# The forget heads of a mixer: probabilities normalised before their turn, values as the stationary operand

## The chip, the cores and the metric

The kernel runs on one core of a Trainium2 chip. The metric is device time in microseconds (us) of one execution. TensorE (PE in the rows) multiplies, VectorE (DVE) and ScalarE (ACT) do elementwise work and move results out of PSUM, GpSimd (POOL) and SyncE (SP) have small parts here; SP issues nearly all weight loads.

## What is computed

Two blocks, one behind the other, on 256 tokens of width 1024. The first block has two layers. Each layer has a mixer with three groups of heads: four differential heads ("diff", eight softmax units of 128 values), four forget heads ("fox", 64 values each) and four retention heads. Then comes a feed-forward part, dense in layer 0 and a mixture of eight experts in layer 1. Only the forget heads change:

```python
def causal_block_attention(q, k, v, scale, cum_logf=None):
    ...
        s = jnp.einsum('bhqd,bhkd->bhqk', q_i, k).astype(jnp.float32) * scale
        if cum_logf is not None:
            s = s + blk[2][..., :, None] - cum_logf[:, :, None, :]
        s = jnp.where(k_pos[None, :] <= q_pos[:, None], s, NEG_INF)
        w = jax.nn.softmax(s, axis=-1).astype(v.dtype)
        return jnp.einsum('bhqk,bhkv->bhqv', w, v)
...
    o_b = merge_heads(causal_block_attention(qb, kb, vb, FOX_DIM ** -0.5, cum))
    return jnp.concatenate([o_a, o_b, o_c], axis=-1) @ w_out
```

## The kernel before, in words

Weights arrive as pieces of 1 MB. ScalarE rounds each piece to a high part (`split`, L1479), VectorE subtracts to get a low part (L2040), and every wide product is three matmuls, high by high, low by high, high by low (`exact`, L758 to L760). Three pieces are held in parts at once; an engine asks for the next piece in program order (`splits`). Each engine runs its own program strictly in its written order and waits on semaphores.

The mixer of a layer is in `attention1`, once per engine, and runs the twelve units of `RUN1` (eight diff units, then fox 0 to 3) as a software pipeline with the step number `i`. On TensorE, step `i` issues the scores of units `i` and `i+1` (at even `i`), turns the probabilities of unit `i-1` (`turn`, L873, three transposes), multiplies unit `i-2` with its values (`values`, L882), and then, up to step 9, a part of a projection (`rows_half` or `feature`, L758 to L760). On VectorE, step `i` takes the row maxima of unit `i` (L2222), at steps 3, 5, 7, 9 finishes a diff head (`diff_out`, L2241 to L2246), at step 9 rotates the retention heads' queries and keys (L2395 to L2400), at step 10 scales the diff rows (L2269), and up to step 8 ends with the low part of a piece (L2040). On ScalarE, step `i` makes the exponentials and row sums of unit `i` (`exps`, L1587), copies the turned probabilities of unit `i-1` out of PSUM (`copy_turned`, L1597), and up to step 10 ends with the high part of a piece (L1479).

Behind the pipeline come the retention heads: scores (`ret_score`, L994, L995), weights made on VectorE (`weigh`, L2299) behind one more low part, and `ret_values` (L1002 to L1005), which wait for `weigh`. The rows of the mixer's result, `y1`, are turned in four blocks of 256 features (`turn_y`, L729; blocks 0 and 1 diff, 2 fox, 3 retention), taken as high and low parts (`turned_y`), and multiplied with the output weights (`output(l, c, j)`, twelve matmuls of L758 to L760 each, for block `c` and column half `j`). Behind step 13, `mixed` issues what is left of them.

For a fox unit, before the change: the exponentials stay unnormalised, are turned, and are then the stationary operand of three products per unit with 64 columns of values moving. The result has tokens on the partitions; when all four units are done, VectorE takes the reciprocals (L2311), scales the whole bank into `y1` (L2312), and TensorE turns these rows with `turn_y(l, 2)`.

## Time and profile before

| | us |
|---|---|
| median of 3 runs | 1936.92 |
| lowest, highest | 1936.78, 1942.82 |
| profiled execution, its own time | 1937.35 |
| its span | 1935.6 |
| PE busy | 1901.9 (98%) |
| VectorE busy, ScalarE busy | 1517.2 (78%), 1261.2 (65%) |
| mean granted TensorE clock | 0.997 |

The mixers' last parts lie at 96 to 140 us (layer 0) and 448 to 493 us (layer 1) of the span. In a timeline row the start says when the first instruction of the row began; matmuls are pipelined, so the step from one row's start to the next one's is what a row takes of TensorE's time, and the length printed is longer than that. The clock column is the granted clock as a share of full speed, 1.00 for 2.4 GHz and 0.50 for 1.2 GHz.

### The profile page before, as it was taken

How to read it: one execution, taken by the hardware profiler on the slowest of the kernel's cores; microseconds unless marked ns; L12 is line 12 of the kernel's file. 1: busy time of each engine (PE TensorE's matmuls, PEld its weight loads, DVE VectorE, ACT ScalarE, POOL GpSimd, SP SyncE). 2: the span in 40 equal slices, each digit the busy share in tenths (PEclk: the TensorE clock that was granted, in tenths of full speed). 3: DMA queues.
4: the chain of work that ended last, by engine and by line, in shares of the span. 5: the costliest groups of instructions: out<-in, count | busy, mean ns of one | idle time of the engine just before them, and what ended most of it. 6: DMA issues, size and time to landing. Idle time of an engine off the chain costs nothing.

```text
span 1935.6 us, 28198 instructions
## 1 busy us (share of the span) xinstructions
PE 1901.9 (98%) x10499; PEld 1614.6 (83%) x10499; DVE 1517.2 (78%) x1792; ACT 1261.2 (65%) x1678; POOL 40.4 (2%) x30
## 2 busy tenths in 40 slices
PE   8999999999899999999999999999999999999999
PEld 7879998888688888888888888888877788788977
DVE  5575555657789989899898989989898875878575
ACT  5654544555777878787787778878777556454553
POOL 0000000000000000000000000000120000000000
PEclk9999999999999999999999999999999999999999
DMA  7717555430899999999999999999996553355421
GB/s 249 250 49 263 180 190 175 153 131 15 315 366 383 365 389 364 391 386 366 393 360 391 366 390 387 364 392 363 390 398 231 172 175 109 131 174 178 149 88 45
DMA packets 246215, 514.38 MB, mean 266 GB/s; under 512 B 12516, under 2 KB 59368, under 8 KB 246120
## 3 DMA queue, kind: packets, MB, share of 16 engines
q1 hardware_dynamic: 242936, 502.48, 72.1%
q0 software_dynamic: 2896, 10.49, 1.4%
q8 instruction: 64, 1.05, 0.2%
q14 instruction: 31, 0.25, 0.0%
q10 hardware_dynamic: 288, 0.11, 0.0%
HBM read 507.27 MB, written 5.77 MB: 265 GB/s over the span
## 4 chain that ended last, share of the span: by engine, by line
PE 85%; DVE 9%; ACT 3%; DMA 1%; issue 1%; ACTq 0%; DVEq 0%
PE bank L758 26%; PE bank L760 26%; PE bank L759 26%; DVE low L2040 2%; DVE low L2640 2%; PE bank L729 1%; PE bank L1180 1%; PE bank L882 1%; DMA scr<-expert_rows,kept_row 1%; ACT high L1479 1%; PE bank L873 1%; PE bank L851 1%; DVE atD L2851 1%; DVE kT L2875 0%; DVE qT L2874 0%
## 5 line engine op out<-in xcount | busy, mean ns | idle before, releaser
L2640 DVE TENSOR_TENSOR low<-raw,high 128x1024 fp32r<-128x1024 f32 x672 | 783.8, 1220 | 72.9 <-ACT high L1683 71.3
L1683 ACT ACTIVATE high<-raw 128x1024 fp32r<-128x1024 f32 x336 | 357.3, 1063 | 206.7 <-PE bank L760 202.2
L2040 DVE TENSOR_TENSOR low<-raw,high 128x2048 fp32r<-128x2048 f32 (+1 forms) x138 | 310.4, 2259 | 164.5 <-ACT high L1479 164.1
L1479 ACT ACTIVATE high<-raw 128x2048 fp32r<-128x2048 f32 (+1 forms) x138 | 260.6, 1894 | 158.6 <-PE bank L760 147.3
L758 PE MATMUL bank<-high,xg_hi 128*128 128x512 f32 x896 | 353.6, 395 | 1.3 <-DVE xg_lo L2620 1.3
L1684 ACT ACTIVATE high<-raw 128x1024 fp32r<-128x1024 f32 x336 | 351.7, 1047 | 0.0
L760 PE MATMUL bank<-high,xg_lo 128*128 128x512 f32 x896 | 349.5, 390 | 0.0
L759 PE MATMUL bank<-low,xg_hi 128*128 128x512 f32 x896 | 348.8, 389 | 0.0
L758 PE MATMUL bank<-high,xT_hi 128*128 128x512 f32 (+1 forms) x576 | 227.4, 395 | 2.5 <-DVE xT_lo L2062 1.3
L760 PE MATMUL bank<-high,xT_lo 128*128 128x512 f32 (+1 forms) x576 | 221.5, 385 | 0.0
L759 PE MATMUL bank<-low,xT_hi 128*128 128x512 f32 (+1 forms) x576 | 221.1, 384 | 0.0
L758 PE MATMUL bank<-high,hT_hi 128*128 128x512 f32 x536 | 209.7, 391 | 1.7 <-DVE hT_lo L2652 1.7
L759 PE MATMUL bank<-low,hT_hi 128*128 128x512 f32 x536 | 208.7, 389 | 0.0
L760 PE MATMUL bank<-high,hT_lo 128*128 128x512 f32 x536 | 208.7, 389 | 0.0
L760 PEld LDWEIGHTS bank<-high,xg_lo 128*128 128x128 f32 x896 | 168.2, 188 | 35.8
L758 PEld LDWEIGHTS bank<-high,xg_hi 128*128 128x128 f32 x896 | 168.2, 188 | 35.1 <-issue 1.6
L759 PEld LDWEIGHTS bank<-low,xg_hi 128*128 128x128 f32 x896 | 168.4, 188 | 33.8
L758 PE MATMUL bank<-xT_hi,high 128*128 128x256 f32 x672 | 192.4, 286 | 3.5 <-issue 1.9
L759 PE MATMUL bank<-xT_lo,high 128*128 128x256 f32 x672 | 190.8, 284 | 0.0
L760 PE MATMUL bank<-xT_hi,low 128*128 128x256 f32 x672 | 190.8, 284 | 0.0
L758 PEld LDWEIGHTS bank<-xT_hi,high 128*128 128x128 f32 x672 | 129.6, 193 | 5.0 <-issue 2.2
L759 PEld LDWEIGHTS bank<-xT_lo,high 128*128 128x128 f32 x672 | 129.6, 193 | 0.4
(357 smaller groups left out, 2309.9 us busy)
## 6 DMA issues: line engine op xcount, KB each, us to landing
raw<-in_moe_w_gate SPq DMA_DIRECT2D x112, 1024.0 KB, 8.9
raw<-in_moe_w_up SPq DMA_DIRECT2D x112, 1024.0 KB, 8.6
raw<-in_moe_w_down SPq DMA_DIRECT2D x112, 1024.0 KB, 8.2
raw<-in_w_in SPq DMA_DIRECT2D x63, 1024.0 KB, 5.3
raw<-in_w_out SPq DMA_DIRECT2D x20, 1024.0 KB, 5.0
raw<-in_dense_w_gate SPq DMA_DIRECT2D x11, 1024.0 KB, 5.4
raw<-in_dense_w_up SPq DMA_DIRECT2D x11, 1024.0 KB, 5.3
raw<-in_dense_w_down SPq DMA_DIRECT2D x11, 1024.0 KB, 5.1
```

The costliest lines, as they stand in the source:

```text
L729: last = pe.transpose(bank_of(key)[:, (k * NT + t) * P:(k * NT + t + 1) * P], rows[:, t, (2 * j + k) * P:(2 * j + k + 1) * P], ident[:, :])
L758: pe.matmul(dst, stationary[0], moving[0], start=start, stop=False)
L759: pe.matmul(dst, stationary[0], moving[1], start=False, stop=False)
L760: return pe.matmul(dst, stationary[1], moving[0], start=False, stop=stop)
L851: pe.matmul(bank[(g + i) % 2][:, c0:c0 + n], q[:, tok(t)], k[:, 0:n], start=(t == 0), stop=False)
L873: last = pe.transpose(bank[2 + g % 2][:, b * P:(b + 1) * P], probs[:, g % 2, b * P:(b + 1) * P], ident[:, :])
L882: last = pe.matmul(att_out(name, u, t), probsT[:, g % 2, c0 + s * P:c0 + (s + 1) * P], val[:, s, :], start=(s == 0), stop=(s == n // P - 1))
L1479: act.activation(high[:, slot, 0:k * n], raw[:, raw_slot[piece], 0:k * n], ACT.Copy).then_inc(high_done, 1)
L1683: act.activation(part[:, 0:HALF // 2], raw[:, slot, 0:HALF // 2], ACT.Copy).then_inc(s["high_half"], 1)
L1684: act.activation(part[:, HALF // 2:HALF], raw[:, slot, HALF // 2:HALF], ACT.Copy).then_inc(s["high"], 1)
L2040: dve.tensor_tensor(low[:, slot, 0:k * n], src, high[:, slot, 0:k * n].bitcast(F32), ALU.subtract).then_inc(low_done, 1)
L2640: last = dve.tensor_tensor(low_part[:, cols], raw[:, at0 + k % slots, cols], high_part[:, cols].bitcast(F32), ALU.subtract)
```

## The change

The four fox units are handled in another way. VectorE normalises each unit's probabilities in place (`fox_rows`: a reciprocal of two row sums, and two in-place scalings of 128x128 and 128x256), and `turn` of a fox unit now waits for that (`fox_scaled`) instead of for the exponentials. The values of two units are multiplied together (`fox_values`): a unit's values are the stationary operand, 64 columns wide, and its turned probabilities move, 256 and 128 columns; one unit writes partitions 0 to 63 of bank 4 and the other 64 to 127. The result already has features on the partitions, so the scaling into `y1` (L2311, L2312), the mark behind it and `turn_y(l, 2)` go, and the block is read from bank 4. On ScalarE, the high part of that block is moved ahead of the gate's Silu. The numbers of two semaphores are counted anew.

```diff
--- before.py
+++ after.py
@@ -418,7 +419,7 @@
             unit(("qcT", l), "act", on=6)
             unit(("kcT", l), "act", on=7)
             for j in range(4):
-                unit(("yT", l, j), "dve", on=(0, 0, 6, 7)[j])
+                unit(("yT", l, j), "dve", on=(0, 0, 4, 7)[j])
             chunk(("wo", l), rows_of(io["w_out"][l], 0, KB))
             if l == 0:
                 places = plan_front(("ffn", l), [("dg", 0), ("du", 0)], True, 4)
@@ -510,7 +511,6 @@
                 att_first[name, l], att_n = att_n, att_n + n
             for k in range(4):
                 out_use["diff", l, k] = len(out_use)
-            out_use["fox", l] = len(out_use)
             out_use["ret", l] = len(out_use)
             out_use["wo", l] = len(out_use)
             if l == 0:
@@ -866,7 +866,11 @@
 
             def turn(name, g):
                 spans = att_shape(name)[2]
-                pe.wait_ge(att_exp, g + 1)
+                if name == "fox":
+                    fox_no = g - att_first["fox", 0]
+                    pe.wait_ge(fox_scaled, fox_no + 1 if fox_no < 4 else g - att_first["fox", 1] + 5)
+                else:
+                    pe.wait_ge(att_exp, g + 1)
                 if g >= 2:
                     pe.wait_ge(att_copied, g - 1)
                 for b in range((spans[1][0] + spans[1][1]) // P):
@@ -882,6 +886,19 @@
                         last = pe.matmul(att_out(name, u, t), probsT[:, g % 2, c0 + s * P:c0 + (s + 1) * P],
                                          val[:, s, :], start=(s == 0), stop=(s == n // P - 1))
                 last.then_inc(att_pv, 1)
+
+            def fox_values(l, p):
+
+
+                turned = att_first["fox", l] + 2 * p
+                pe.wait_ge(att_copied, turned + 2)
+                for s in range(NT):
+                    for i in range(2):
+                        cols = slice(0, SEQ) if s == 0 else slice(SEQ, 3 * P)
+                        last = pe.matmul(bank[4][64 * i:64 * i + 64, p * SEQ + s * P:(p + 1) * SEQ],
+                                         v[:, s, 512 + 64 * (2 * p + i):576 + 64 * (2 * p + i)],
+                                         probsT[:, (turned + i) % 2, cols], start=(s == 0), stop=(s == NT - 1))
+                last.then_inc(*((att_pv, 2) if p == 0 else (unit_full, 1)))
 
             def attention1(l):
 
@@ -915,9 +932,13 @@
                             pe.wait_ge(out_taken, out_use["diff", l, max(0, u // 2 - 1)])
                             if u == 4:
                                 emptied(pe, ("forgetT", l))
-                        if (name, u) == ("fox", 0):
-                            pe.wait_ge(out_taken, out_use["diff", l, 3])
-                        values(name, u, first + i - 2)
+                        if name == "diff":
+                            values(name, u, first + i - 2)
+                        elif u % 2 == 1:
+                            if u == 1:
+                                pe.wait_ge(out_taken, out_use["diff", l, 3])
+                                free_bank(pe, ("yT", l, 2))
+                            fox_values(l, u // 2)
                     if i < 10:
                         name = ("va", "vfb", "qkb", "qkc", "vgc")[i // 2]
                         if name == "qkb":
@@ -941,7 +962,7 @@
                         pe.wait_ge(att_exp, first + 11)
                         turn_y(l, 0)
                     if i == 12:
-                        pe.wait_ge(out_taken, out_use["fox", l])
+                        pe.wait_ge(out_taken, out_use["ret", l])
                         ret_values(l, 0)
                         ret_values(l, 1)
                         ret_score(l, 2)
@@ -953,6 +974,8 @@
                         output(l, 0, 0)
                 ret_values(l, 2)
                 ret_values(l, 3)
+                filled(pe, ("yT", l, 2))
+                pe.nop().then_inc(att_pv, 2)
 
             def attention2(l):
 
@@ -1006,7 +1029,7 @@
                           start=False, stop=True).then_inc(ret_pv, 1)
 
             def turn_y(l, j):
-                pe.wait_ge(y_ready, 3 * l + max(1, j))
+                pe.wait_ge(y_ready, 2 * l + (2 if j == 3 else 1))
                 turn_rows(("yT", l), y1, [j])
 
             def output(l, c, j):
@@ -1032,7 +1055,6 @@
                 output(l, 1, 0)
                 pe.wait_ge(att_copied, att_first["fox", l] + 4)
                 output(l, 0, 1)
-                turn_y(l, 2)
                 output(l, 1, 1)
                 emptied(pe, ("yT", l, 2))
                 output(l, 2, 0)
...
@@ -1916,11 +1938,11 @@
                 attention1(l)
 
                 turned_y(l, 1)
+                turned_y(l, 2)
                 emptied(act, ("vgc", l, 1))
                 act.activation(sg[:, :, :], sg[:, :, :], ACT.Silu).then_inc(gates_in, 1)
                 sqrt_ahead()
                 serve_sqrt(8)
-                turned_y(l, 2)
                 splits(pieces_of["wo", l][0])
                 turned_y(l, 3)
                 splits(last_piece["wo", l] - 1)
@@ -2247,12 +2269,25 @@
                                                         in1=ya[:, t, hd, :], op0=ALU.mult, op1=ALU.add)
                     last.then_inc(out_taken, 1)
 
+                def fox_rows(u):
+
+
+                    dve.wait_ge(att_exp, att_first["fox", l] + u + 1)
+                    r = rinv[:, 2 * u:2 * u + 2]
+                    link(dve.reciprocal(r, rowsum[:, 2 * u:2 * u + 2]))
+                    for t, (c0, n) in enumerate(att_shape("fox")[2]):
+                        rows = probs[:, (att_first["fox", l] + u) % 2, c0:c0 + n]
+                        last = dve.tensor_scalar(rows, rows, r[:, t:t + 1], None, ALU.mult)
+                    last.then_inc(fox_scaled, 1)
+
                 for i in range(len(RUN1)):
                     if i == 5:
                         take_scaled(("qkb", l, 0), qT[:, 4:6, :], 0.125)
                     if i == 6:
                         take_scaled(("qkb", l, 1), kT[:, 4:6, :])
                     maxima(*RUN1[i], first + i)
+                    if i >= 9:
+                        fox_rows(i - 9)
                     if i in (3, 5, 7, 9):
                         diff_out((i - 3) // 2)
                     if i == 5:
@@ -2299,6 +2334,7 @@
                     dve.tensor_tensor(ret_w[:, u, :], bank[6 + u % 2][:, 0:3 * P], decay[:, u, :],
                                       ALU.mult).then_inc(ret_weights, 1)
 
+                fox_rows(3)
                 splits(pieces_of["vgc", l][0])
                 weigh(0)
                 weigh(1)
@@ -2307,14 +2343,7 @@
                 weigh(2)
                 weigh(3)
                 turned_y(l, 1)
-                dve.wait_ge(att_pv, first + len(RUN1))
-                link(dve.reciprocal(rinv[:, 0:8], rowsum[:, 0:8]))
-                dve.tensor_tensor(y1[:, :, 512:768].rearrange("p t (h n) -> p h t n", h=4),
-                                  bank[4][:, :].rearrange("p (h t n) -> p h t n", h=4, t=NT),
-                                  per(rinv[:, 0:8].rearrange("p (h t) -> p h t", h=4), 64),
-                                  ALU.mult).then_inc(out_taken, 1)
-                dve.wait_ge(out_taken, out_use["fox", l] + 1)
-                mark().then_inc(y_ready, 1)
+                turned_y(l, 2)
 
             def attention2(l):
 
@@ -2476,7 +2505,6 @@
                 ycf = y1[:, :, 768:1024]
                 dve.wait_ge(gates_in, l + 1)
                 dve.tensor_tensor(ycf, ycf, sg[:, :, :], ALU.mult).then_inc(y_ready, 1)
-                turned_y(l, 2)
                 splits(pieces_of["wo", l][0])
                 turned_y(l, 3)
                 splits(last_piece["wo", l] - 2)
```

VectorE, steps 9 and 10 of layer 0, from the maxima of fox 1 on. Before:

```order
L2222 TENSOR_REDUCE negmax<-bank 128x1
L2241 RECIPROCAL rinv<-rowsum 128x4 [waits att_pv]
L2242 TENSOR_SCALAR rinv<-rinv,lam 128x2 [waits dve_step]
L2244 TENSOR_TENSOR yf<-bank,rinv 128x2x128 [waits dve_step]
L2246 SCALAR_TENSOR_TENSOR yf<-bank,rinv,yf 128x128 [waits dve_step]
L2246 SCALAR_TENSOR_TENSOR yf<-bank,rinv,yf 128x128
L2105 TENSOR_SCALAR stat<-ysum 128x8 [waits diff_squares_summed]
```

The same place in the change:

```order
L2244 TENSOR_REDUCE negmax<-bank 128x1
L2277 RECIPROCAL rinv<-rowsum 128x2 [waits att_exp]
L2280 TENSOR_SCALAR probs<-probs,rinv 128x128 [waits dve_step]
L2280 TENSOR_SCALAR probs<-probs,rinv 128x256
L2263 RECIPROCAL rinv<-rowsum 128x4 [waits att_pv]
L2264 TENSOR_SCALAR rinv<-rinv,lam 128x2 [waits dve_step]
L2266 TENSOR_TENSOR yf<-bank,rinv 128x2x128 [waits dve_step]
L2268 SCALAR_TENSOR_TENSOR yf<-bank,rinv,yf 128x128 [waits dve_step]
```

The normalisation of fox 0 stands behind the maxima of fox 1 and ahead of the last diff head.

VectorE, from the maxima of fox 3 on, before (`low` is the low part of a piece, `ret_w` the retention weights):

```order
L2222 TENSOR_REDUCE negmax<-bank 128x1 [waits att_scores]
L2222 TENSOR_REDUCE negmax<-bank 128x1
L2040 TENSOR_TENSOR low<-raw,high 128x2048 [waits high_parts_done]
L2299 TENSOR_TENSOR ret_w<-bank,at 128x384 [waits ret_scores] x2
L2062 SCALAR_TENSOR_TENSOR xT_lo<-bank,y_gain,xT_hi 128x256 [waits high_rows_taken]
```

In the change:

```order
L2244 TENSOR_REDUCE negmax<-bank 128x1 [waits att_scores]
L2244 TENSOR_REDUCE negmax<-bank 128x1
L2277 RECIPROCAL rinv<-rowsum 128x2 [waits att_exp]
L2280 TENSOR_SCALAR probs<-probs,rinv 128x128 [waits dve_step]
L2280 TENSOR_SCALAR probs<-probs,rinv 128x256
L2277 RECIPROCAL rinv<-rowsum 128x2 [waits att_exp]
L2280 TENSOR_SCALAR probs<-probs,rinv 128x128 [waits dve_step]
L2280 TENSOR_SCALAR probs<-probs,rinv 128x256
L2062 TENSOR_TENSOR low<-raw,high 128x2048 [waits high_parts_done]
L2334 TENSOR_TENSOR ret_w<-bank,at 128x384 [waits ret_scores] x2
L2084 SCALAR_TENSOR_TENSOR xT_lo<-bank,y_gain,xT_hi 128x256 [waits high_rows_taken]
```

The low part and the retention weights now stand behind the normalisation of fox 3, which waits for its exponentials.

TensorE, the turn of fox 3 and what follows, before:

```order
L873 MATMUL bank<-ident,probs 128x128 [waits att_copied,att_exp]
L873 MATMUL bank<-ident,probs 128x128 x2
L882 MATMUL bank<-v,probsT 128x64 [waits att_copied]
L882 MATMUL bank<-v,probsT 128x64 x2
L1002 MATMUL bank<-v,ret_w 128x64 [waits ret_weights,out_banks_taken]
```

In the change:

```order
L877 MATMUL bank<-ident,probs 128x128 [waits att_copied,fox_rows_scaled]
L877 MATMUL bank<-ident,probs 128x128 x2
L1025 MATMUL bank<-v,ret_w 128x64 [waits ret_weights,out_banks_taken]
```

The values of fox 2 are gone from here; the first retention product, with its wait for the weights, follows the turn at once.

## Rows read from the trace of the kernel before

**Rows 1.** The page, busy time of each engine.
```profile
PE 1901.9 (98%) x10499; PEld 1614.6 (83%) x10499; DVE 1517.2 (78%) x1792; ACT 1261.2 (65%) x1678; POOL 40.4 (2%) x30
```

**Rows 2.** Timeline of TensorE, layer 0; columns: start us, us, instruction, idle before.
```profile
96.10 0.49 PE L873 MATMUL bank<-ident,probs 128*128 128x128 f32 x3
...
102.66 0.93 PE L851 MATMUL bank<-kT,qT 64*128 64x128 f32 x8
103.51 1.58 PE L858 MATMUL bank<-yf,ident 128*128 128x128 f32 x8
104.92 0.39 PE L863 MATMUL bank<-causal,ident_one 128*128 128x128 bf16 x4
...
111.64 0.55 PE L873 MATMUL bank<-ident,probs 128*128 128x128 f32 x3 [1.09 <-ACT probs L1587]
...
112.74 0.39 PE L1002 MATMUL bank<-v,ret_w 128*128 128x64 f32 x2
...
115.45 0.47 PE L758 MATMUL bank<-high,xT_hi 128*128 128x512 f32 x1
...
118.30 0.78 PE L882 MATMUL bank<-v,probsT 128*128 128x64 f32 x6
118.91 0.39 PE L1002 MATMUL bank<-v,ret_w 128*128 128x64 f32 x2
...
125.80 0.60 PE L729 MATMUL bank<-ident,yf 128*128 128x128 f32 x4
126.16 0.48 PE L758 MATMUL bank<-high,xT_hi 128*128 128x512 f32 x1
```

**Rows 3.** Timeline of VectorE, layer 0.
```profile
96.03 2.29 DVE L2040 TENSOR_TENSOR low<-raw,high 128x2048 fp32r<-128x2048 f32 x1 [3.17 <-ACT high L1479]
...
98.78 0.17 DVE L2241 RECIPROCAL rinv<-rowsum 128x4 f32<-128x4 f32 x1
...
105.24 0.62 DVE L2222 TENSOR_REDUCE negmax<-bank 128x1 f32<-128x128 f32 x2
105.78 1.22 DVE L2269 TENSOR_TENSOR yf<-yf,stat 128x1024 f32<-128x1024 f32 x1
...
107.44 2.28 DVE L2040 TENSOR_TENSOR low<-raw,high 128x2048 fp32r<-128x2048 f32 x1
109.99 1.02 DVE L2299 TENSOR_TENSOR ret_w<-bank,at 128x384 f32<-128x384 f32 x2 [0.27 <-PE bank L995]
```

**Rows 4.** Timeline of ScalarE, layer 0.
```profile
108.34 0.65 ACT L1576 ACTIVATE kT<-bank 128x512 f32<-128x512 f32 x1
108.82 1.97 ACT L1479 ACTIVATE high<-raw 128x2048 fp32r<-128x2048 f32 x1
110.62 0.42 ACT L1587 ACTIVATE probs<-bank,negmax 128x128 f32<-128x128 f32 x1
```

**Rows 5.** Groups of VectorE by line and form: busy us, mean ns.
```profile
L2841 DVE TENSOR_SCALAR kT<-kT,lbs 128x256 f32<-128x256 f32 x8 | 2.7, 340 | 0.0
```

**Rows 6.** Timeline of layer 1, TensorE and VectorE.
```profile
448.05 0.49 PE L873 MATMUL bank<-ident,probs 128*128 128x128 f32 x3
...
450.75 0.17 DVE L2241 RECIPROCAL rinv<-rowsum 128x4 f32<-128x4 f32 x1
```

**Rows 7.** Timeline of TensorE, second block, products 64 columns wide side by side.
```profile
1644.85 1.15 PE L1358 MATMUL bank<-qT,kT 128*64 128x64 f32 x32
1645.93 0.50 PE L758 MATMUL bank<-high,xT_hi 128*128 128x512 f32 x1
```

**Rows 8.** Stretches: busy us of PE, PEld, DVE, ACT, POOL; clock; DMA share; GB/s.
```profile
11.80:15.20 3.40, 3.40 (x19) 3.40 (x18) 2.33 (x6) 2.90 (x5) 0.00 (x0) 0.51 1.10 348
...
466.40:468.70 2.30, 2.30 (x13) 1.92 (x13) 2.02 (x3) 0.00 (x0) 0.00 (x0) 0.50 0.00 0
```

**Rows 9.** Timeline of TensorE, the idle time ahead of the two low stretches.
```profile
10.55 0.35 PE L758 MATMUL bank<-xT_hi,high 128*128 128x256 f32 x1 [1.90 <-issue]
...
463.62 0.55 PE L873 MATMUL bank<-ident,probs 128*128 128x128 f32 x3 [1.08 <-ACT probs L1587]
```

More of the change, by code:

```diff
@@ L311, in program @@
         gates_in = sem("hgrn_gates_in")
+        fox_scaled = sem("fox_rows_scaled")
         hid_high, hid_ready = sem("hidden_high_ready"), sem("hidden_ready")
@@ L1387, in hgrn @@
                 heads(bank[4 + 2 * ((LEVELS + 1) % 2)], 0, 1).then_inc(hg_scores, 1)
-                pe.wait_ge(y_ready, 3 * LAYERS + 2 * l + 1)
+                pe.wait_ge(y_ready, 2 * LAYERS + 2 * l + 1)
                 turn_rows(("yT2", l), y2, (0, 1))
@@ L1437, in after_experts @@
                         if c == 3:
-                            pe.wait_ge(y_ready, 3 * LAYERS + 2 * l + 2)
+                            pe.wait_ge(y_ready, 2 * LAYERS + 2 * l + 2)
                             turn_rows(("yT2", l), y2, (2, 3))
```

## The prediction

> **What bounds the kernel now.** I read the page first: TensorE is busy 98% of the span [rows 1]. It is so by its own matmuls nearly everywhere, so whatever makes TensorE wait, or work longer, is paid in full. Then I went to the timeline of the one place that the change touches, the last steps of the mixer's pipeline, in layer 0 and in layer 1. Three things are to be seen there. TensorE turns fox 0 at 96.10 without idle time ahead of it, and waits only once in the tail, 1.09 us for the exponentials of fox 3 [rows 2]. VectorE is late against it: the low part of a piece starts at 96.03 because VectorE stood 3.17 us waiting for the high part, and only at 98.78 is VectorE through with the maxima of fox 1 [rows 3]. Layer 1 is the same picture, turn at 448.05, VectorE free at 450.75 [rows 6]. So TensorE is ahead of VectorE by 2.7 us at this point, and that costs nothing now because the turn of fox 0 needs only ScalarE.
>
> **The change, part by part**, in the times of layer 0.
>
> *Work taken off TensorE.* The four transposes of block 2 go: 125.80 to 126.16, 0.36 us, and with the shorter first matmul behind them some 0.44 [rows 2]. The values of a fox unit took 0.61 (118.30 to 118.91) [rows 2], 1.2 for two. Two units in the new form stream 768 columns. Full width, as many columns took 1.41 us (L858, 103.51 to 104.92); in two row halves of the array at once 0.85 (L851, 102.66 to 103.51) [rows 2]. Column halves are used elsewhere: 32 records of 64 columns in 1.08 us, 34 ns each [rows 7], against 0.10 us for a record of `values` (six in 0.61) [rows 2], so halves do overlap. I take 0.85, with 0.6 and 1.41 as ends: 0.35 less for each pair. The first pair stands where TensorE will wait anyway, so it is worth nothing. The second takes the place of one unit's 0.61 behind `output(l, 0, 0)`: 0.24 more there (0 to 0.8). On the path: 0.24 - 0.44 = -0.2 a layer.
>
> The Trainium skill, "TensorEngine Tiling (Array Packing)", section "Theoretical Speedup", states up to 2x for a small dimension of 64. By it and the new column count the pair would take half of 1.41, and the text's sum would be lower by 0.15 us a layer; rows 7 agree with an overlap.
>
> *Work taken off VectorE.* The reciprocals, the scaling of the bank and the mark go, about 1 us behind the last piece of the pipeline. VectorE's chain for the retention rows then starts when the last retention product is done, and the turn of block 3 comes four `output` blocks later; cover enough, I cost it at nothing.
>
> *Work put on VectorE.* A normalisation is a reciprocal of 0.17 [rows 3] and two scalings in SBUF, at most 0.34 each [rows 5]; pipelined I take 0.75. There are four a layer, and what counts is where they stand.
>
> *First wait.* The turn of fox 0 now needs the normalisation that follows the maxima of fox 1: 98.78 + 0.75 = 99.5, against 96.10. TensorE stops for 3.4 to 3.5 us with the values of diff 7, half of the last projection piece and the next scores queued behind it. In layer 1 it is 450.75 + 0.75 against 448.05, again 3.5. The diff head behind it on VectorE shifts by 1.6, its rotation ends at about 107.3 instead of 105.2, which the later scores hide.
>
> *What follows.* The scores of fox 2 came 2.58 us after 102.66 (maxima at 105.24) [rows 2, 3]; now 106.16 + 2.58 = 108.7. Maxima 0.54, normalisation of fox 1 0.75: the turn of fox 1 at 110.0, a second wait of about 1.2. Then L2269 (1.13 to the next), maxima of fox 3, normalisation of fox 2: 112.4, a third wait, about 1. ScalarE cannot make the exponentials of fox 3 before two moves of turned retention rows and a high part. TensorE's eight transposes (0.11 each by rows 2) end at 111.4, the second move (0.5) at 111.9, the high part (108.82 to 110.62, 1.8 us) at 113.7, the exponentials 1.02 later (110.62 to 111.64) at 114.8 [rows 2, 4]. Normalisation of fox 3: 115.5, where the turn was at 111.64.
>
> *The one that ends last.* VectorE's next instruction is the low part of a piece, and only then come the retention weights. Before, the low part ran at 107.44, under everything else, and the weights at 109.99 [rows 3]. Now it is behind fox 3: 115.5 + 2.2 = 117.7, first weights 118.25, first retention product at 118.3 against 112.74 [rows 2]. From there to `output(l, 0, 0)` it was 2.71 us (112.74 to 115.45) [rows 2], and nothing in it waits for more. So TensorE is 5.56 us late there, and dense behind it. With the -0.2 of above: **5.4 us a layer, 10.7 for both**.
>
> *The clock.* The granted clock stood at 1.2 GHz (0.51, 0.50) in two stretches shown, 11.8 to 15.2 and 466.4 to 468.7 [rows 8]; before the first TensorE had been idle 1.90 us, before the second 1.08 us in a stretch of short matmuls [rows 9]. In layer 0 the same 1.09 us brought no fall. A stop of 3.5 us is longer than any of these, and the second group of waits adds about 5 us of idle in 10. A stretch like 11.8 to 15.2 costs dense matmuls half of 3.4, so up to 1.7 us. I take 1.2 for the first stop of each layer (part of the slow time may fall on waits) and 1.2 for the second group; layer 1 has its slow stretch already, 1.2 to 1.7 us of loss, so there the second is no addition: 1.2 + 1.2 + 1.2 = 3.6, less 0.5 for the chance that one stays away, **3.1**. The ends are -1.7 (none anywhere, the present one gone as well) and +8 (two or three in each layer, fully paid).
>
> The Trainium skill, "TensorE: Matmul & The Clock Gate", section "What's actually happening", calls the throttled clock the default state that activity releases; the 0.51 behind 1.90 us of idle time agrees. By this rule the sum keeps the clock's part; without it the sum is 10.7.
>
> **The sum.** 10.7 + 3.1 = 13.8 on the profiled execution's 1937.35 (span 1935.6) gives 1951.2. The median of the runs, 1936.92, is 0.4 lower; predicted median: 1950.8.
>
> **The rivals.**
>
> *A, the forecast*: waits of TensorE for the normalisation, with loss of clock. 1947.5 to 1957. Chance 0.66.
>
> *B, the waits without new slow stretches*: sum between 10.7 - 1.7 and 10.7, 1945.9 to 1947.6. For it: layer 0 kept its clock over 1.09 us of idle time. Against: 1.90 us was enough. Chance 0.16.
>
> *C, the other side: the normalisation is hidden.* If VectorE reached it before TensorE reached the turn, TensorE would keep the savings: 0.35 + 0.44 + 0.35 a layer, some 2.3 us in both, and 1934.6, within 0.3% of before. The point from which it decides is the 2.7 us by which VectorE is late at 98.78; its low part there is bound by ScalarE's high part and not by TensorE, so nothing in the change moves it. Chance 0.08. The Trainium skill, "TensorEngine Tiling (Array Packing)", section "Theoretical Speedup", taken alone would lead here; it is a rule for the products, not for their waits.
>
> *D, only the latency of the normalisations is paid*: 0.75 for each of eight, 6.0, less the same 2.3 of work saved: +3.7, 1940.6. This needs each to start when its exponentials end. The order of VectorE speaks against it for fox 0 (exponentials long done when VectorE comes) and for the low part behind fox 3. Chance 0.10.
>
> **How the numbers follow.** A difference of 0.3%, 5.8 us, is about what a measurement of this kernel can tell from none. A and B lie above it at all their values; of C and D all lies within. A little is left for a gain that I do not see. Slower 0.83, same 0.14, faster 0.03. The range runs from 1944 (B, with a second wait smaller than worked out) to 1957.5 (A with slow stretches near the upper end); C and D are the 2 in 10 left out.
>
> **What would show it.** Right: in the changed trace the turn of fox 0 has 3 to 3.5 us idle ahead of it, released by VectorE, in both layers; the first retention product waits over 2 us for the retention weights; the low part between the two normalisations and the weights starts near 115.5; the granted clock falls behind 99 and behind 451. The pair of values takes 0.6 to 0.9. Wrong: no idle ahead of the turn of fox 0, or VectorE through with the normalisation of fox 0 before 97; a pair of values at 1.4; `output(l, 0, 0)` less than 4 us later than 115.45. A delay that is there at 121 but gone by 140 would mean that what follows the mixer had waits of its own which absorb it.

## The result, and the profile after

| | before | changed |
|---|---|---|
| median us (4 runs each) | 1937.28 | 1958.75 |
| lowest, highest | 1936.78, 1942.82 | 1956.31, 1960.08 |
| profiled execution, span | 1935.6 | 1957.2 |
| granted TensorE clock, mean | 0.997 | 0.991 |

The ratio is 1.0100, 95% interval 1.0087 to 1.0113: slower, by some 20 us. The median lies 1.25 us above the end of the predicted range; the ratio on the predicted basis (1936.92) gives 1956.3. All further runs of before, 64 in four batches, had medians of 1938.1 to 1939.1, so the loss is some 20 us (17 to 22 by the interval). Each ratio below is to runs of before taken together with that kernel.

The page of the changed kernel. TensorE is as full as before by its share, which hides the loss.

```profile
PE 1909.8 (98%) x10475; PEld 1618.1 (83%) x10475; DVE 1520.2 (78%) x1810; ACT 1263.0 (65%) x1678; POOL 38.8 (2%) x30
```

The waits of TensorE in the changed kernel (us in total, times, longest us). The first and the third line are new.

```profile
PE bank L877 <- DVE probs L2280: 11.4, 7, 3.3
PE bank L729 <- DMA gcols<-in_l_gain_columns: 5.0, 1, 5.0
PE bank L1025 <- DVE ret_w L2334: 3.5, 2, 2.2
```

TensorE, layer 0, answering to [rows 2]. The turns of fox 0 to 2 have 3.30, 1.26 and 0.90 us of idle time ahead of them, all released by the normalisation, and the first retention product has 1.29 us, released by the retention weights (2.21 in layer 1).

```profile
99.74 0.55 PE L877 MATMUL bank<-ident,probs 128*128 128x128 f32 x3 [3.30 <-DVE probs L2280]
...
108.02 0.93 PE L851 MATMUL bank<-kT,qT 64*128 64x128 f32 x8
...
111.93 0.55 PE L877 MATMUL bank<-ident,probs 128*128 128x128 f32 x3 [1.26 <-DVE probs L2280]
...
114.25 0.76 PE L877 MATMUL bank<-ident,probs 128*128 128x128 f32 x3 [0.90 <-DVE probs L2280]
114.94 1.55 PE L898 MATMUL bank<-probsT,v 128*64 128x256 f32 x8
116.41 1.23 PE L1017 MATMUL bank<-qT,kT 64*128 64x256 f32 x4
...
120.24 0.41 PE L1025 MATMUL bank<-v,ret_w 128*128 128x64 f32 x2 [1.29 <-DVE ret_w L2334]
...
127.43 0.87 PE L898 MATMUL bank<-probsT,v 128*64 128x256 f32 x8
128.23 0.43 PE L1025 MATMUL bank<-v,ret_w 128*128 128x64 f32 x2
...
140.59 0.60 PE L729 MATMUL bank<-ident,yf 128*128 128x128 f32 x4
```

VectorE, layer 0, answering to [rows 3]. The order does what the listing said: low part, maxima of fox 1, then fox 0's normalisation; further down the last normalisation waits 2.48 us for its exponentials, and the low part and the weights wait behind it.

```profile
96.20 2.29 DVE L2062 TENSOR_TENSOR low<-raw,high 128x2048 fp32r<-128x2048 f32 x1 [3.17 <-ACT high L1501]
98.41 0.62 DVE L2244 TENSOR_REDUCE negmax<-bank 128x1 f32<-128x128 f32 x2
98.95 0.15 DVE L2277 RECIPROCAL rinv<-rowsum 128x2 f32<-128x2 f32 x1
99.14 0.55 DVE L2280 TENSOR_SCALAR probs<-probs,rinv 128x128 f32<-128x128 f32 x2
...
116.67 0.17 DVE L2277 RECIPROCAL rinv<-rowsum 128x2 f32<-128x2 f32 x1 [2.48 <-ACT probs L1609]
116.88 0.55 DVE L2280 TENSOR_SCALAR probs<-probs,rinv 128x128 f32<-128x128 f32 x2
117.34 2.28 DVE L2062 TENSOR_TENSOR low<-raw,high 128x2048 fp32r<-128x2048 f32 x1
119.54 1.01 DVE L2334 TENSOR_TENSOR ret_w<-bank,at 128x384 f32<-128x384 f32 x2
```

Stretches of the changed kernel (busy us of PE, PEld, DVE, ACT, POOL; granted clock; DMA share; GB/s), first three of layer 0, then three of layer 1. Behind each 3.3 us wait and behind the wait for the retention weights the clock stands partly at 1.2 GHz: 8.3 us at 0.79, 7.2 at 0.76, 9.3 at 0.70, 7.2 at 0.76. The last two rows are cut out of the first stretch of each layer and show the level itself; layer 0 has a third slow stretch, from 114 to 118 us, inside its 12.2 us at 0.86.

```profile
99.70:108.00 8.30, 8.26 (x33) 6.56 (x33) 5.49 (x12) 3.27 (x8) 2.01 (x1) 0.79 0.39 125
108.00:120.20 12.20, 8.79 (x58) 6.21 (x57) 7.02 (x17) 8.27 (x20) 0.00 (x0) 0.86 0.00 0
120.20:127.40 7.20, 7.16 (x36) 5.97 (x36) 5.24 (x8) 0.84 (x2) 0.00 (x0) 0.76 0.01 2
...
460.40:469.70 9.30, 9.29 (x35) 7.57 (x35) 5.49 (x12) 3.24 (x8) 2.01 (x1) 0.70 0.01 2
469.70:481.90 12.20, 7.41 (x58) 5.38 (x58) 7.05 (x17) 8.32 (x20) 0.00 (x0) 1.00 0.00 0
481.90:489.10 7.20, 7.19 (x36) 5.88 (x36) 5.21 (x8) 0.84 (x2) 0.00 (x0) 0.76 0.00 0
...
101.00:104.00 3.00, 3.00 (x8) 2.35 (x8) 2.12 (x7) 1.40 (x5) 0.42 (x1) 0.50 0.76 264
461.00:465.00 4.00, 4.00 (x15) 3.42 (x14) 1.50 (x6) 1.28 (x6) 0.00 (x0) 0.50 0.02 4
```

**Where the time went.** One measure serves for all kernels below: the *tail* of a layer, from the moment at which TensorE is ready to turn fox 0 to the start of the turn of block 3. Before: 96.10 to 131.73, 35.63 us, and 448.05 to 485.24, 37.19 us. Changed: 96.44 (99.74 less 3.30) to 140.59, 44.15 us, and 457.10 to 502.30, 45.20 us. So 8.5 us and 8.0 us are lost in the two tails. From the turn of block 3 in layer 1 to the end it is 1450.4 us before and 1454.9 changed, 4.5 us more over instructions that are the same. The first tail starts 0.34 us later, and 0.19 us more lie between the two tails; with these 0.5 us that is the 21.6 us between the spans.

### The profile page after: what moved, and what is told of

The parts are those of the page before. It is cut to its first block, busy times and chain, and to the rows that moved or that the text cites. A ratio compares the mean times of both kernels' runs of the same rounds, so it can differ in the third digit from the quotient of the medians.

```text
span 1957.2 us, 28168 instructions
## 1 busy us (share of the span) xinstructions
PE 1909.8 (98%) x10475; PEld 1618.1 (83%) x10475; DVE 1520.2 (78%) x1810; ACT 1263.0 (65%) x1678; POOL 38.8 (2%) x30
## 4 chain that ended last, share of the span: by engine, by line
PE 84%; DVE 10%; ACT 3%; DMA 2%; issue 1%; ACTq 0%; SPq 0%; DVEq 0%
PE bank L758 26%; PE bank L760 25%; PE bank L759 25%; DVE low L2062 3%; DVE low L2668 2%; PE bank L729 1%; PE bank L1202 1%; ACT high L1501 1%; DMA scr<-expert_rows,kept_row 1%; PE bank L886 1%; PE bank L877 1%; PE bank L851 1%; DVE atD L2879 1%; DVE kT L2903 0%; DVE qT L2902 0%
## 5 line engine op out<-in xcount | busy, mean ns | idle before, releaser
L758 PEld LDWEIGHTS bank<-high,xT_hi 128*128 128x128 f32 x576 | 109.4, 190 | 25.8 <-DVE xT_lo L2084 1.7
```

What stands on the lines that cost most here:

```text
L758: pe.matmul(dst, stationary[0], moving[0], start=start, stop=False)
```

## The experiments

**1. Only fox 0 earlier.** In the change's VectorE program:

```diff
-                    if i >= 9:
-                        fox_rows(i - 9)
+                    if i == 8:
+                        fox_rows(0)
+                    if i >= 10:
+                        fox_rows(i - 9)
```

> Only the normalisation of fox 0 is moved, from behind the maxima of fox 1 to behind the maxima of fox 0, where VectorE stands 3.17 us in the trace of before. If the order of VectorE is what costs, the 3.30 us wait of TensorE ahead of the turn of fox 0 goes in both layers, and with it the slow clock that follows it: 3.3 to 5 us a layer less than the change, about 1949 to 1952. If the new products or the added VectorE work cost by themselves, the time stays at 1957 to 1959.

Measured 1949.39 us (1948.18 to 1950.74), ratio to before 1.0059 (1.0043 to 1.0076). Tails 40.56 and 41.08 us: 3.6 and 4.1 less than the change. The first wait is gone (the turn starts at 96.34 with no idle time), and the clock behind it stays up, 1.00 from there to the turn of fox 1 in both layers. What stays is the other end; TensorE of this kernel, layer 0:

```profile
112.69 0.55 PE L877 MATMUL bank<-ident,probs 128*128 128x128 f32 x3 [0.74 <-DVE probs L2280]
115.45 0.66 PE L1025 MATMUL bank<-v,ret_w 128*128 128x64 f32 x2 [2.21 <-DVE ret_w L2336]
```

**2. All four moved.** Fox 0 as in 1; fox 1 behind the last diff head of step 9, where VectorE waits for ScalarE; fox 2 behind the maxima of fox 3; and

```diff
-                fox_rows(3)
                 splits(pieces_of["vgc", l][0])
                 weigh(0)
                 weigh(1)
+                fox_rows(3)
```

> All four normalisations stand where VectorE is idle or nothing waits behind them: fox 0 behind its maxima, fox 1 behind the last diff head, fox 2 behind the maxima of fox 3, fox 3 behind the first two retention weights. Order theory: nearly all of the 21 us goes; TensorE keeps one wait of 1.5 to 1.9 us for fox 3 and one of some 0.6 for fox 2, and has 0.2 us less work a layer: 1936 to 1940, the same as before. Rival (work costs by itself): still above 1950.

Measured 1939.95 us (1938.00 to 1942.80, 10 runs), ratio 1.0004 (0.9994 to 1.0014): no difference from before. Tails 35.48 and 35.47 us. The same VectorE work, the same products and the same output form as the change, and the loss is gone: only its order made it. Two waits for the normalisation are left, TensorE of layer 0:

```profile
109.89 0.55 PE L877 MATMUL bank<-ident,probs 128*128 128x128 f32 x3 [0.93 <-DVE probs L2280]
...
113.85 0.55 PE L877 MATMUL bank<-ident,probs 128*128 128x128 f32 x3 [1.17 <-DVE probs L2280]
```

**3. The waits filled.** In `turn`, for the fox units, ahead of the wait for the normalisation:

```diff
+                    pe.wait_ge(att_copied, g - 1)
+                    for _ in range((14, 5, 4, 0)[u]):
+                        pe.matmul(bank[2 + g % 2][:, :], xT_hi[:, 6, 0:P],
+                                  xT_hi[:, 6:8, :].rearrange("p a b -> p (a b)"), start=True, stop=True)
```

> The change, with TensorE multiplying for nothing while it waits for the normalisations of fox 0, 1 and 2: 14, 5 and 4 fp32r matmuls of 512 columns into the bank that the turn then overwrites, about 3.2, 1.1 and 0.9 us. The waits stay as long, but the engine is busy in them. If the slow clock behind the waits is a part of the loss (6 us at the mixers, more behind the routing), the clock stays at 2.4 GHz there and the time falls by 4 to 9 us, to 1950 to 1955, though TensorE does more work. If the waits alone make the loss, the time stays at 1958 or rises by up to 1.

Measured 1954.40 us (1951.55 to 1956.28), ratio 1.0079 (1.0062 to 1.0095). TensorE computes 46 matmuls more and the program is 4.3 us faster than the change at the medians, as the clock theory says. The lowest run of the change (1956.31) lies above the highest here (1956.28), but the two 95% intervals of the ratios overlap, so the size is rough. The stretches of layer 0, the first of them the filled wait:

```profile
97.40:100.90 3.50, 3.35 (x15) 2.44 (x14) 3.41 (x6) 0.68 (x3) 0.00 (x0) 1.00 0.34 96
100.90:107.50 6.60, 6.60 (x33) 5.38 (x33) 4.41 (x11) 3.23 (x8) 2.02 (x1) 1.00 0.49 156
107.50:119.70 12.20, 9.54 (x67) 6.85 (x66) 8.11 (x19) 8.32 (x20) 0.00 (x0) 0.97 0.00 0
119.70:128.30 8.60, 8.56 (x38) 7.16 (x38) 5.24 (x8) 0.84 (x2) 0.00 (x0) 0.64 0.01 2
```

The clock behind the first wait is 1.00 where the change had 0.79, and the same work takes 6.6 us in place of 8.3; in layer 1 it is 6.6 us at 1.00 against 9.3 at 0.70. But behind the wait that was not filled, for the retention weights, it now falls on dense work, 8.6 us at 0.64 where the change had 7.2 at 0.76. So the tails gain little, 44.04 and 44.28 us (97.42 to 141.46, 457.86 to 502.14), 0.1 and 0.9 less than the change; 2.5 us of the gain of this trace lie behind the mixers (1452.4). The effect on the clock is shown; that it is worth 4 us by the first waits alone is not.

**4. The kernel before, with the change's waits.** Its own products, its own scaling of the bank and its turn of block 2; `turn` waits for `fox_scaled`, and `fox_rows` stands where the change has it, with

```diff
-                        last = dve.tensor_scalar(rows, rows, r[:, t:t + 1], None, ALU.mult)
+                        last = dve.tensor_scalar(rows, rows, 1.0, None, ALU.mult)
```

> The kernel before with its own products, its scaling of the bank and its turn of block 2, but with the four pieces of VectorE work at the places of the change (the scalings multiply by 1.0) and the turns waiting for them. Order theory: as slow as the change or up to 1 us slower, since 0.2 to 0.5 us a layer of TensorE work is not saved: 1957 to 1961. If the new products (64 columns stationary, two heads side by side) or the shorter end cost instead, this stays near 1937.

Measured 1959.27 us (1958.18 to 1961.78), ratio 1.0113 (1.0096 to 1.0130): as slow as the change. Tails 46.17 and 45.76 us, 2.0 and 0.6 more than the change, where 0.2 to 0.5 were expected. Together with 2 this settles the cause: the added VectorE steps in these places, with the waits for them, bring the whole loss without the new products, and with the steps placed otherwise the new form of the forget heads costs nothing.

**5. Fox 0 and fox 3 moved**, fox 1 and 2 as in the change.

> As with fox 0 moved early, and now the normalisation of fox 3 also moved, from ahead of the low part and the retention weights to behind the first two weights. Fox 1 and fox 2 stay where the change has them. Order theory: the wait of 2.2 us ahead of the first retention product goes; some 2 us a layer less, 1944 to 1947. If instead the loss that is left after fox 0 is all in fox 1 and fox 2, this stays at 1949.

Measured 1940.82 us (1938.08 to 1942.65, 10 runs), ratio 1.0012 (1.0002 to 1.0021). That is 8.6 us less than 1, where some 4 were expected (1944 to 1947). Tails 37.48 and 35.92 us, 3.1 and 5.2 less than in 1. The wait for the weights is gone (2.2 us in layer 0 and 1.7 in layer 1 of kernel 1), and so is the slow clock behind it, which the expectation had not counted. What fox 1 and fox 2 cost where the change has them is the rest to 2: 0.45 us in layer 1 (35.92 against 35.47); in layer 0 there is a slow stretch at 108 to 112 us in this trace, which makes 2.0.

**6. The two heads of a pair one after the other**, on top of 2.

```diff
-                for s in range(NT):
-                    for i in range(2):
+                for i in range(2):
+                    for s in range(NT):
```

> The version with all four normalisations moved, and the two heads of a pair of values issued one after the other (both products of a head, then both of the next) in place of alternating. If the column halves of the array overlap only for neighbouring products of different heads, a pair goes from 0.80 us to 1.1 to 1.4 us of TensorE's time. The total moves by 0.6 to 1.2 us at most, within the noise of the runs: read the pair, not the total. If halves do not overlap at all, nothing changes in the pair.

Measured 1938.04 us (1936.21 to 1943.52, 10 runs), ratio 1.0000 (0.9991 to 1.0010). The pair (109.21 to the next start) takes 0.81 us, as with alternating heads (110.36 to 111.16 in 2, 0.80). The overlap doesn't need products of different heads next to each other.

```profile
109.21 0.88 PE L898 MATMUL bank<-probsT,v 128*64 128x256 f32 x8
110.02 0.49 PE L1017 MATMUL bank<-qT,kT 64*128 64x256 f32 x2
```

It does not follow that halves don't overlap. The trace of before has products of 64 columns that use one half only (`corner_scores`, L1367), 16 records in 1.07 us, 67 ns each, against 34 ns each where both halves have work (32 records in as much time) [rows 7]:

```profile
1673.62 1.15 PE L1367 MATMUL bank<-qT,kT 128*64 128x64 f32 x16
1674.69 0.50 PE L758 MATMUL bank<-high,xT_hi 128*128 128x512 f32 x1
```

So two halves with work share the time, and in a group of eight records it doesn't matter in what order they are issued.

**7. The tail reordered**, on top of 2: ScalarE's high part of step 10 goes behind the copy of fox 3, so that the exponentials of fox 3 come first, and VectorE's tail is

```diff
-                splits(pieces_of["vgc", l][0])
-                weigh(0)
-                weigh(1)
                 fox_rows(3)
+                weigh(0)
+                weigh(1)
                 turned_y(l, 0)
-                splits(pieces_of["vgc", l][1])
+                splits(pieces_of["vgc", l][0])
                 weigh(2)
                 weigh(3)
                 turned_y(l, 1)
+                splits(pieces_of["vgc", l][1])
                 turned_y(l, 2)
```

> The version with all four moved, and ScalarE's exponentials of fox 3 issued ahead of the high part that stood in front of them (the high part goes behind the copy of fox 3), the normalisation of fox 3 at once behind that of fox 2, and VectorE's two low parts of the tail behind the retention work that TensorE waits for. Worked out from the trace of the moved version: the wait of 1.17 us ahead of the turn of fox 3 goes, the output products start 1.2 us earlier in each layer; 2 to 3 us less than the moved version, and 1 to 2.5 us less than before: 1934.5 to 1937 where before is at 1937 to 1938. If the tail is bound elsewhere, the same as the moved version.

Measured 1937.37 us (1934.95 to 1941.65, 11 runs), ratio 0.9995 (0.9986 to 1.0005). Tails 34.13 and 34.14 us, 1.3 less than 2 in each, and the wait ahead of the turn of fox 3 is gone. At the end of 1937 us this cannot be told from before; 1 to 2.5 us less were expected.

**8. The kernel before, exponentials of fox 3 first.** One change, in ScalarE's program:

```diff
-                    if 1 <= i <= 10:
+                    if 1 <= i <= 9:
                         splits(pieces_of[("va", "vfb", "qkb", "qkc", "vgc")[(i - 1) // 2], l][(i - 1) % 2])
+                    if i == 11:
+                        splits(pieces_of["vgc", l][1])
```

> The kernel before with one thing changed: ScalarE's exponentials of fox 3 ahead of the high part of step 10. In its trace TensorE waits 1.09 us for them in each layer. If that wait is on the path, 1.1 us a layer go, and with it perhaps the slow clock at 466 us in layer 1 (up to 1.7): 2 to 4 us less than before. It tells how much of the reordered tail's gain comes from ScalarE's order alone, without the new form of the forget heads.

Measured 1937.20 us (1933.72 to 1938.14, 11 runs), ratio 0.9995 (0.9986 to 1.0004). Tails 34.29 and 34.29 us: 1.3 less in layer 0, and 2.9 in layer 1, where the slow stretch at 466 us [rows 8] does not come. The tails lose what was expected, 4.2 us together; of the 2 to 4 us expected in the total the medians show 1.0, which is not clear of noise. So nearly all of 7's gain over before is ScalarE's order. The new form of the forget heads as placed in 7 gains 34.29 less 34.13, 0.16 us a layer. Its work is not that small: TensorE is busy for 33.98 us of the tail in kernel 8 and for 32.59 in kernel 7, 1.4 us less. But TensorE is idle for 0.31 us of the tail in kernel 8 and for 1.54 in kernel 7, nearly all of it in two waits, 0.59 us for ScalarE ahead of the turned retention rows and 0.93 us for the normalisation of fox 2. They take back most of the work saved. Stretches of layer 0 (us of the stretch, then TensorE's busy us), kernel 7 and then kernel 8:

```profile
97.22:131.35 34.13, 32.59 (x195) 26.20 (x194) 28.76 (x52) 18.87 (x40) 2.02 (x1) 1.00 0.13 40
...
96.34:130.63 34.29, 33.98 (x207) 28.49 (x206) 27.94 (x46) 18.54 (x40) 2.02 (x1) 1.00 0.13 40
```

**9. The kernel before again**, for a second trace.

> The kernel before, unchanged, for a second trace. The stretch from the last turned block of layer 1 (485.6 us) to the end took 1450.0 us in the first trace of before and 1454.6 in that of the change, which is the same code from there on. If that part differs by chance from execution to execution, this trace may fall anywhere from 1450 to 1455; the first 485.6 us should come out within 2 us of the first trace. If the later part is always 1450 here, the 4.6 us belong to the change.

Measured 1937.69 us, span 1935.9. Tails 35.59 and 37.16 us, the later part 1450.5. The tails repeat to 0.04 us. The later part repeats here too, so on two traces of before its 1450.4 looks firm. But over the other kernels, whose instructions are the same from there on, it took 1450.6 (6 and 8), 1450.7 (4), 1451.3 (5), 1451.6 (7), 1452.3 (1), 1452.4 (3), 1454.9 (the change) and 1455.1 (2). Kernel 4, as late at the mixers as the change, has 1450.7, and kernel 2, as early as before, has 1455.1: it doesn't follow the delay.

**10. Retention values first**, on top of 7: ScalarE copies the retention values ahead of its wait for the rotation, and only the gate's copies behind it.

> The version with the reordered tail, and ScalarE taking the retention values out of PSUM ahead of its wait for the rotation, where it stands 2.4 us, so that only the gate's two copies (0.36 us each) are left ahead of the exponentials of fox 2. Those come 0.7 us earlier. TensorE's two waits that are left in that version, 0.59 us ahead of the turned retention rows and 0.93 us ahead of the turn of fox 2, shrink by 0.7 us together: a layer's stretch from the turn of fox 0 to the turned block 3 goes from 34.13 to about 33.4 us. The total: 1.4 us less than the reordered tail, 2 to 6 us less than before, 1932 to 1936.5. If the stretch does not shrink, the exponentials were not what fox 2 waited for.

Measured 1936.98 us (1932.89 to 1939.85, 12 runs), ratio 0.9993 (0.9984 to 1.0001), the lowest median of all, above the 1932 to 1936.5 expected and still not clear of before. Tails 33.91 and 33.92 us, 0.22 less than 7 and not 0.7. TensorE, layer 0:

```profile
107.00 1.06 PE L955 MATMUL bank<-ident,a 128*128 128x128 f32 x8 [0.24 <-ACT sg L1650]
109.34 0.55 PE L877 MATMUL bank<-ident,probs 128*128 128x128 f32 x3 [1.28 <-DVE probs L2283]
```

The first wait fell from 0.59 to 0.24 as meant, the second grew from 0.93 to 1.28. Ahead of the normalisation of fox 2, VectorE still has the scaling of the diff rows and the maxima of fox 3, and these now end last; that was read from the order and the durations, and not tried.

| kernel | median us | tail, layer 0 | tail, layer 1 | from there to the end |
|---|---|---|---|---|
| before | 1937.28 | 35.63 | 37.19 | 1450.4 |
| changed | 1958.75 | 44.15 | 45.20 | 1454.9 |
| 1 fox 0 early | 1949.39 | 40.56 | 41.08 | 1452.3 |
| 2 all moved | 1939.95 | 35.48 | 35.47 | 1455.1 |
| 3 waits filled | 1954.40 | 44.04 | 44.28 | 1452.4 |
| 4 before with waits | 1959.27 | 46.17 | 45.76 | 1450.7 |
| 5 fox 0 and 3 | 1940.82 | 37.48 | 35.92 | 1451.3 |
| 6 heads in turn | 1938.04 | 35.51 | 35.49 | 1450.6 |
| 7 tail reordered | 1937.37 | 34.13 | 34.14 | 1451.6 |
| 8 before, exponentials first | 1937.20 | 34.29 | 34.29 | 1450.6 |
| 10 values first | 1936.98 | 33.91 | 33.92 | 1450.5 |

## Why the prediction was right, and where it was not

**First wait.** Forecast 3.4 to 3.5 us in both layers; 3.30 and 3.31. The normalisation took 0.79 us from its first start to the turn (98.95 to 99.74), forecast 0.75. The step is right, and kernel 1 shows it on the chip.

**What follows.** Forecast waits of 1.2 and about 1 ahead of fox 1 and fox 2; 1.26 and 0.90. The price of their places alone is small, 0.45 us by kernel 5.

**The one that ends last.** Forecast: the retention weights behind the low part behind fox 3, the first retention product 22.2 us after the turn of fox 0 was due (118.3 less 96.1) at full clock. Measured 23.8 (120.24 less 96.44) and 24.8 (481.91 less 457.10). What is over is the slow clock behind the first wait: 8.3 us at 0.79 are 1.7 us lost, 9.3 us at 0.70 are 2.8. Take them off and 22.1 and 22.0 are left. The 5.56 us of the forecast stand. Of its signs, a wait of over 2 us ahead of the first retention product came in layer 1 only (2.21; 1.29 in layer 0). There the slow stretch from 114 to 118 us fell into slack: from the turn of fox 1 to the first retention product both layers take 8.31 us (111.93 to 120.24, 473.60 to 481.91), so that stretch cost nothing.

**Work taken off TensorE.** The pair took 0.80 us (127.43 to 128.23), forecast 0.85 between 0.6 and 1.41. All that the new form takes off is 1.4 us a layer by kernel 7 against 8; rival C had 1.14 (0.35, 0.44 and 0.35). The forecast's 0.2 is what it takes to be left on the path of the change. No run measures that by itself: the 0.16 us of 7 against 8 come close to it, but as 1.4 us of work less waits that the forecast of the change has elsewhere, so that agreement is luck. The reason given, halves overlapping, holds by L1367 against L1358; the forecast's own comparison, 34 ns against 0.10 us for a record of `values`, overstated it, since a record in one half alone takes 67. The Trainium skill, "TensorEngine Tiling (Array Packing)", section "Key Properties", says that different tiles can load weights and multiply in parallel; 34 against 67 ns agrees.

**The clock: the term that was mis-sized.** Forecast 3.1 us net for both layers, 1.2 for each new slow stretch. In the two tails, 8.5 and 8.0 less 5.4 each leave 3.2 and 2.6 us, so 5.8. The clock column gives about as much by another way: 1.7 and 2.8 behind the first waits, 1.7 in each layer behind the wait for the weights (7.2 us at 0.76), less the 1.6 that layer 1 of before had already (37.19 less 35.63), 6.3. Against that the forecast had 1.2 and 1.2, then 1.2 in all for the second, less 0.5 for the chance that one stays away; all came. The stretch behind the first wait fell nearly wholly on dense matmuls; I had taken part of it to fall on waits. The Trainium skill, "TensorE: Matmul & The Clock Gate", section "What's actually happening", has activity release the throttle, and kernel 3, where matmuls without use kept 1.00, agrees.

**What was left out.** I put nothing behind the mixers. There the trace of the change has 4.5 us more than that of before. By stretches of 4 us from 504 us on, the clock took 5.1 us in the change (524 to 532 and 548 to 556 us) and 1.7 before (504 to 512), which is 3.4 of the 4.5; TensorE was also idle 1.3 us longer there (22.2 us against 20.9). These slow stretches lie at the experts' routing, where TensorE has short waits in every kernel. They come and go between kernels that share this code: measured in the same way up to 560 us, the clock took 1.7 us in before, 4, 6, 7, 8, 9 and 10 (that part 1450.4 to 1451.6 us), 3.4 in 1, 3 and 5 (1451.3 to 1452.4), and 5.1 in 2 and the change (1455.1, 1454.9). So most of the spread of that part goes with what the clock took, in steps of 1.7 us. How much of it is in the medians, and what decides when the clock falls there, stays open. Before, and then kernel 2:

```profile
504.00:512.00 8.00, 6.10 (x40) 5.89 (x41) 6.70 (x21) 5.68 (x11) 1.15 (x2) 0.79 0.65 233
...
504.00:516.00 12.00, 9.57 (x50) 8.93 (x51) 9.32 (x30) 6.94 (x15) 1.50 (x2) 0.72 0.73 266
532.00:540.00 8.00, 6.31 (x25) 5.35 (x26) 6.85 (x12) 3.98 (x6) 0.82 (x1) 0.79 1.00 347
```

**The sum.** 10.7 of waits, 5.8 of clock in the tails, 4.5 behind, 0.5 at the starts: 21.5 of the 21.6 us between the spans. The 5.8 is what the 10.7 leave of the tails, so that this adds up proves little; what bears it out is the 22.1 and 22.0 above and the 6.3 of the clock column. The forecast had 10.7 and 3.1, 13.8 in all: the waits and their causes came as said, and the time was 7.8 us short, by the clock in the tails and by what lies behind them. The rivals: B (no slow clock) falls by the windows; C (normalisation hidden) and D (latency only) fall by the waits of 3.3 and 2.2 us. Kernel 2 is the nearest to C: no difference that a measurement can tell, as C said. But its waits of 0.93 and 1.17 us are not hidden, and the 1934.6 us of C did not come (1939.95).

## What to carry to other kernels

A piece of work put between two engines costs what its place in the third engine's program makes it cost: 0.75 us of VectorE work behind the wrong instruction stopped TensorE for 3.3 us, and the same work one step earlier, in VectorE's own idle time, cost nothing. Before inserting such a step, read when the engine that is to do it gets there and what queues behind it, not how long it takes. Each stop of TensorE can be paid a second time by the slower clock on the dense work behind it, here 1.7 and 2.8 us on 3.3; and a form that takes 1.4 us of work off TensorE in each layer gained 0.16 us of time, since TensorE then waits for the others.

## What the runs showed of the hardware

- Products with a stationary operand of 64 columns cost 67 ns a record in one column half and 34 with both in use; a pair of heads of 768 fp32 columns takes 0.80 us in either issue order, against 1.41 us for as many columns at full width [rows 2].
- With a wait of 3.2 to 3.3 us ahead of the turn of fox 0 the clock fell to 1.2 GHz in both layers, in the change (0.50 at 101 to 104 and 461 to 465 us) and in kernel 4, and in neither layer where matmuls without use filled that wait (kernel 3). After 1.1 us of idle time among short matmuls it fell in layer 1 in both traces of before and in layer 0 in neither; with that wait gone (kernel 8) it fell in neither layer. Kernel 2 has waits of 0.93 and 1.17 us at nearly the same place, and it fell in neither layer there.
- The tails repeat to 0.04 us between two traces of the same kernel. The part behind them, the same instructions in all kernels, took 1450.4 to 1455.1 us, and the first tail started at 95.3 to 97.5 us; that, not the tails, sets how small a gain can be measured here: tails shorter by 4.5 to 5 us in sum (7, 10) moved the medians by about 1.
